# Early norms one row-block per attention round, and parts of the output projection moved into the attention drain

## What is computed

```
h = rmsnorm(x) * (1 + sc1) + sh1                      # and the same for the context
a, s, qkv = split(h @ w_in)
y = concat(short_conv(a), spatial_gating(s), neighbourhood_attention(qkv))   # 256 + 256 + 512 columns
y = group_rmsnorm(y, out_norm_g, 16 groups of 64) @ w_out
x = x + g1 * y
h2 = rmsnorm(x) * (1 + sc2) + sh2                     # then PEER: queries, top-k, experts, final norm
```

## Time and profile before

| what | value |
|---|---|
| runs of the kernel | 944.63, 945.29, 946.36 us; median 945.29 us |
| the profiled execution | 940.76 us, of it 939.0 us from the first to the last instruction |
| PE busy, PE weight load busy | 890.5 us (95%), 837.9 us (89%) |
| DVE, ACT, POOL busy | 535.4, 283.5, 257.4 us |
| mean granted TensorE clock | 0.976 of full |
| read from HBM | 290.72 MB, 311 GB/s over the span |

### The profile page before, as it was taken

How to read it: one execution, slowest core, us unless ns; L and a number is a source line. 1 busy time by engine, 2 the same in 40 slices (tenths; PEclk the granted TensorE clock), 3 DMA queues, 4 the chain that set the end, 5 groups by cost and what they waited for, 6 DMA issues and landing times.

```text
span 939.0 us, 18081 instructions
## 1 busy us (share of the span) xinstructions
PE 890.5 (95%) x6850; PEld 837.9 (89%) x6850; DVE 535.4 (57%) x1035; ACT 283.5 (30%) x687; POOL 257.4 (27%) x239
## 2 busy tenths in 40 slices
PE   5799999869999999999998999999999999999995
PEld 3587998449798999999997999999999999999995
DVE  1446104657458976997445688888434343334347
ACT  3453223664633211112113688883000000000002
POOL 0000000330133033346543233364432323222320
PEclk9597999999999999999999899999999999999998
DMA  9674583204336489999999999999999999999993
GB/s 371 289 269 171 189 314 136 89 7 175 135 135 270 119 244 384 410 409 409 409 409 410 409 362 326 320 320 353 408 409 408 409 409 409 409 409 409 409 409 131
DMA packets 73984, 292.74 MB, mean 312 GB/s; under 512 B 9026, under 2 KB 9154, under 8 KB 67396
## 3 DMA queue, kind: packets, MB, share of 16 engines
q1 hardware_dynamic: 36868, 159.67, 44.1%
q0 software_dynamic: 28416, 100.78, 28.4%
q10 hardware_dynamic: 8640, 31.46, 8.4%
HBM read 290.72 MB, written 1.05 MB: 311 GB/s over the span
## 4 chain that ended last, share of the span: by engine, by line
PE 36%; DMA 32%; DVE 5%; ACT 3%; issue 2%; POOL 1%; ACTq 0%; DVEq 0%; SPq 0%
DMA A<-in_peer_v,row_expert 25%; PE bank L830 24%; PE bank L839 4%; DMA A<-in_peer_u,row_expert 4%; DVE sum L1355 3%; DMA stage<-in_peer_u_t 2%; PE bank L573 1%; PE bank L575 1%; PE bank L574 1%; PE bank L724 1%; PE bank L727 1%; PE bank L726 1%; POOL A L1635 1%; PE bank L779 1%; PE bank L757 1%
## 5 line engine op out<-in xcount | busy, mean ns | idle before, releaser
L830 PE MATMUL bank<-A,stage 128*128 128x160 f32 x2048 | 291.3, 301 | 2.3 <-DMA stage<-in_peer_u_t 1.1
L830 PEld LDWEIGHTS bank<-A,stage 128*128 128x128 f32 x2048 | 282.0, 191 | 5.9 <-issue 5.6
L886 PE MATMUL bank<-A,stage 128*128 128x160 f32 x2048 | 278.4, 299 | 0.0
L886 PEld LDWEIGHTS bank<-A,stage 128*128 128x128 f32 x2048 | 278.2, 190 | 0.0
L1355 DVE SCALAR_TENSOR_TENSOR sum<-A,row_gate,sum 128x1024 f32<-128x1024 f32 x81 | 104.0, 1284 | 132.8 <-DMA A<-in_peer_v,row_expert 131.1
L1635 POOL DMA_INDIRECT A<-in_peer_u,row_expert x80 | 91.1, 1138 | 140.7 <-DVE row_dot L1342 133.4
L1635 POOL DMA_INDIRECT A<-in_peer_v,row_expert x84 | 82.6, 984 | 166.2 <-DVE sum L1355 148.8
L1342 DVE CUSTOM_DVE_ANT_0 A<-A 128x1024 f32<-128x1024 f32 x80 | 97.4, 1220 | 46.9 <-DMA A<-in_peer_u,row_expert 46.8
L1175 ACT ACTIVATE A<-bank 128x480 f32<-128x480 f32 x1 | 0.6, 570 | 276.3 <-PE bank L886 276.3
L1108 ACT ACTIVATE A<-bank 128x160 f32 (+1 forms) x88 | 26.7, 303 | 155.2 <-PE bank L830 155.2
L575 PE MATMUL bank<-h_hi,ring_low 128*128 128x256 f32 x256 | 73.1, 286 | 0.0
(11 more groups left out here) (234 smaller groups left out, 1240.6 us busy)
## 6 DMA issues: line engine op xcount, KB each, us to landing
stage<-in_peer_u_t SPq DMA_DIRECT2D x128, 512.0 KB, 11.1
stage<-in_peer_v SPq DMA_DIRECT2D x68, 512.0 KB, 7.7
stage<-in_peer_v ACTq DMA_DIRECT2D x60, 512.0 KB, 8.3
A<-in_ada_w SPq DMA_DIRECT2D x24, 1024.0 KB, 7.0
A<-in_w_in SPq DMA_DIRECT2D x11, 1024.0 KB, 4.8
A<-in_w_q SPq DMA_DIRECT2D x8, 1024.0 KB, 5.5
A<-in_w_out SPq DMA_DIRECT2D x4, 1024.0 KB, 6.9
stage<-in_bias_mask SPq DMA_DIRECT2D x1, 2048.0 KB, 12.7
```

The costliest lines, as they stand in the source:

```text
L830: mm = pe.matmul(o, stage[j][:, k * P:(k + 1) * P], H2[:, k, 0:ND], start=(k == 0), stop=(k == KD - 1))
L886: mm = pe.matmul(bank[b][:, n * ND:(n + 1) * ND], stage[c % SLOTS][:, m * P:(m + 1) * P], A3[:, c, :], start=(c == 0 and n == 0), stop=(c ...
```

## The change

In the attention rounds, DVE norms one row-block in each of rounds 1 to 4 instead of two in rounds 2 and 4; ACT rounds one in each of rounds 2 to 5; DVE takes one rest in each of rounds 4 to 7, two rounds behind the rounding.

In the drain, three pieces of the output projection are taken out of it and put into the list, 96 of its 192 matmuls: `out_part` 0 (k = 0, 1 for output blocks 0 to 3, 24 matmuls) ahead of `attend_pair` 6, `out_part` 1 (k = 2, 3 for the same blocks, 24) behind `turned_pair` 7, and `out_part` 2 (k = 0 to 3 for output blocks 4 to 7, 48) behind `attend_pair` 7. `group` 2 goes between `turned_pair` 7 and `out_part` 1, in another bank. `group` 3 comes behind `out_part` 2. The projection proper keeps k = 4 to 7. DVE norms blocks 4 and 5 when the last heads have been copied, blocks 6 and 7 after the reciprocal of group 3. Quarters 0 to 3, whose rests DVE makes, get a semaphore of their own.

```diff
--- before.py
+++ after.py
@@ -131,18 +131,24 @@
             steps += [("score_pair", j), ("scores", 2 * j), ("scores", 2 * j + 1)]
         if j == 0:
             turn()
+        if j == pairs:
+            steps.append(("out_part", 0))
         if 0 <= j - 2:
             steps.append(("attend_pair", j - 2))
         if 0 <= j - 1 < pairs:
             steps.append(("turned_pair", j - 1))
+        if j == pairs:
+            steps += [("group", 2), ("out_part", 1)]
         if 1 <= j <= 6:
             steps += [("quarter", 2 * j + 2), ("quarter", 2 * j + 3)]
-        if j in (3, 5):
-            steps.append(("yn", j // 2 - 1))
+        if 2 <= j <= 5:
+            steps.append(("yn_round", j - 2))
+        if 4 <= j <= 7:
+            steps.append(("yn_rest", j - 4))
         if j == 6:
             steps.append(("squares", 2))
     q0 = len(splits)
-    steps += [("squares", 3), ("group", 2), ("group", 3), ("yn", 2), ("yn", 3)]
+    steps += [("squares", 3), ("out_part", 2), ("group", 3), ("yn", 2), ("yn", 3)]
     steps += [("split", q0), ("split", q0 + 1), ("split", q0 + 2), ("w_out", 0), ("stat2", 0), ("x1_turned", 0)]
 
     ada(4 * G2)
@@ -233,16 +239,19 @@
             if n % 2 == 0:
                 put(("attend", n // 2), n // 2 % 2)
         elif kind == "group":
-            put((kind, n), 2 + n % 2)
+            put((kind, n), (2, 3, 0, 3)[n])
+        elif kind == "out_part":
+            if n != 1:
+                for m in (n, n + 1):
+                    put(("w_out", m), 4 + m)
         elif kind == "w_out":
-            for m in range(4):
-                put((kind, m), 4 + m)
+            pass
         elif kind == "stat2":
             put((kind, 0), 0)
         elif kind == "x1_turned":
             for j in range(4):
                 put((kind, j), (1, 2, 3, 7)[j])
-        elif kind in ("squares", "split", "context", "ctx_squares", "yn", "quarter", "scores"):
+        elif kind in ("squares", "split", "context", "ctx_squares", "yn", "yn_round", "yn_rest", "quarter", "scores"):
             pass
         elif kind == "keys":
             put((kind, n), 4 + n % 4)
@@ -440,7 +449,8 @@
         weight_rounded, weight_split, h_full, h_rounded, ctx_ready = map(
             sem, ("weight_rounded", "weight_split", "h_full", "h_rounded", "ctx_ready"))
         query_split = sem("query_split")
-        quarter_rounded, quarter_split = sem("quarter_rounded"), sem("quarter_split")
+        quarter_rounded, quarter_split, first_quarter_split = map(
+            sem, ("quarter_rounded", "quarter_split", "first_quarter_split"))
         yn_rounded, yn_split = sem("yn_rounded"), sem("yn_split")
         silu_zero, silu_ready, sq_ready, root_ready, h_ready, mrow_ready = map(
             sem, ("silu_zero", "silu_ready", "sq_ready", "root_ready", "h_ready", "mrow_ready"))
@@ -709,25 +719,34 @@
                 pe.matmul(o[:, :], group_ones, YS[:, 2 * j:2 * j + 2, :], start=True, stop=True)\
                   .then_inc(fill_sem(("group", j)), 1)
 
+            def out_products(k, dims):
+
+                w = [(weight_hi[splits.index(("w_out", b))], WR_lo[:, ring_of[("w_out", b)] % RING]) for b in range(4)]
+                pe.wait_ge(yn_split, k + 1)
+                for m in dims:
+                    name = ("w_out", m // 2)
+                    o = opened(pe, name) if k == 0 and m % 2 == 0 else bank[place[name][0]]
+                    oo, cc = o[:, m % 2 * T:m % 2 * T + T], slice(m % 2 * P, m % 2 * P + P)
+                    a_hi, a_lo = w[m // 2]
+                    pe.matmul(oo, a_hi[:, k, cc], yn_hi[:, k, :], start=(k == 0 and m % 2 == 0), stop=False,
+                              skip_group_check=True)
+                    pe.matmul(oo, a_hi[:, k, cc], YN_lo[:, k, :], start=False, stop=False, skip_group_check=True)
+                    mm = pe.matmul(oo, a_lo[:, k, cc], yn_hi[:, k, :], start=False, stop=(k == KD - 1),
+                                   skip_group_check=True)
+                    if k == KD - 1 and m % 2 == 1:
+                        mm.then_inc(fill_sem(("w_out", m // 2)), 1)
+
+            def out_part(i):
+
+                pe.wait_ge(first_quarter_split, 4)
+                pe.wait_ge(quarter_split, 12 if i == 2 else 4)
+                for k in range(4) if i == 2 else (2 * i, 2 * i + 1):
+                    out_products(k, range(4, KD) if i == 2 else range(4))
+
             def out_projection():
 
-
-                pe.wait_ge(quarter_split, 16)
-                w = [(weight_hi[splits.index(("w_out", b))], WR_lo[:, ring_of[("w_out", b)] % RING]) for b in range(4)]
-                for k in range(KD):
-                    pe.wait_ge(yn_split, k + 1)
-                    for m in range(KD):
-                        name = ("w_out", m // 2)
-                        o = opened(pe, name) if k == 0 and m % 2 == 0 else bank[place[name][0]]
-                        oo, cc = o[:, m % 2 * T:m % 2 * T + T], slice(m % 2 * P, m % 2 * P + P)
-                        a_hi, a_lo = w[m // 2]
-                        pe.matmul(oo, a_hi[:, k, cc], yn_hi[:, k, :], start=(k == 0 and m % 2 == 0), stop=False,
-                                  skip_group_check=True)
-                        pe.matmul(oo, a_hi[:, k, cc], YN_lo[:, k, :], start=False, stop=False, skip_group_check=True)
-                        mm = pe.matmul(oo, a_lo[:, k, cc], yn_hi[:, k, :], start=False, stop=(k == KD - 1),
-                                       skip_group_check=True)
-                        if k == KD - 1 and m % 2 == 1:
-                            mm.then_inc(fill_sem(("w_out", m // 2)), 1)
+                for k in range(4, KD):
+                    out_products(k, range(KD))
 
             def second_stat():
 
@@ -805,10 +824,12 @@
                     turned_pair(n)
                 elif kind == "attend_pair":
                     attend_pair(n)
-                elif kind in ("squares", "split", "context", "ctx_squares", "yn", "quarter", "scores"):
+                elif kind in ("squares", "split", "context", "ctx_squares", "yn", "yn_round", "yn_rest", "quarter", "scores"):
                     pass
                 elif kind == "group":
                     group_sums(n)
+                elif kind == "out_part":
+                    out_part(n)
                 elif kind == "w_out":
                     out_projection()
                 elif kind == "stat2":
@@ -1013,8 +1034,8 @@
                         act.wait_ge(ring_full[0][ring_of[name] % RING], 16 * (ring_of[name] // RING + 1))
                     act.activation(weight_hi[splits.index(name)][:, kk, :], WR[:, ring_of[name] % RING, kk, :],
                                    ACT.Copy).then_inc(quarter_rounded, 1)
-                elif kind == "yn":
-                    for k in (2 * n, 2 * n + 1):
+                elif kind == "yn_round" or kind == "yn":
+                    for k in (n,) if kind == "yn_round" else (2 * n, 2 * n + 1):
                         act.wait_ge(yn_ready, k + 1)
                         act.activation(yn_hi[:, k, :], YN[:, k, :], ACT.Copy).then_inc(yn_rounded, 1)
                 elif kind == "ctx_squares":
@@ -1195,7 +1216,7 @@
             eng.wait_ge(quarter_rounded, n + 1)
             eng.tensor_tensor(WR_lo[:, slot, kk, :], WR[:, slot, kk, :],
                               weight_hi[splits.index(name)][:, kk, :].bitcast(F32), ALU.subtract)\
-               .then_inc(quarter_split, 1)
+               .then_inc(first_quarter_split if n < 4 else quarter_split, 1)
 
         @block.vector
         def _(dve):
@@ -1240,13 +1261,11 @@
                 dve.sem_inc(free_sem(("group", j)), 1)
                 link(dve.reciprocal(roots[j % 2], roots[j % 2]))
 
-            def group_norm(j):
-                for m in range(2):
-                    k = 2 * j + m
-                    dve.scalar_tensor_tensor(YN[:, k, :], YR[:, k, :], colv[:, COL_OG + k:COL_OG + k + 1],
-                                             roots[j % 2][:, m * T:(m + 1) * T], ALU.mult, ALU.mult)\
-                       .then_inc(yn_ready, 1)
-                dve.wait_ge(yn_ready, 2 * j + 2)
+            def norm(k):
+                j, m = k // 2, k % 2
+                dve.scalar_tensor_tensor(YN[:, k, :], YR[:, k, :], colv[:, COL_OG + k:COL_OG + k + 1],
+                                         roots[j % 2][:, m * T:(m + 1) * T], ALU.mult, ALU.mult)\
+                   .then_inc(yn_ready, 1)
 
             def softmax(j):
 
@@ -1434,13 +1453,17 @@
                     if n >= 3 and n % 2 == 1:
                         attended((n - 3) // 2)
 
-                    if n in (2, 4):
-                        group_norm(n // 2 - 1)
+                    if 1 <= n <= 4:
+                        norm(n - 1)
                 elif kind == "squares" and n == 3:
                     attended(3)
+                    norm(4)
+                    norm(5)
                 elif kind == "group":
                     group_reciprocal(n)
-                    group_norm(n)
```

(7 more changed lines are left out.)

## The result

| | before | after |
|---|---|---|
| median of seven runs each, first session | 944.63 us (942.31 to 946.36) | 937.89 us (935.25 to 939.67) |
| ratio of the runs | | 0.9945, 95% interval 0.9928 to 0.9961 |
| profiled execution, and its span | 940.76 us, 939.0 us | 937.84 us, 936.1 us |
| mean granted clock of the profiled execution | 0.976 | 0.976 |

The change makes the kernel faster, by 5.2 us according to the ratio; with its interval the ratio gives 3.7 to 6.8 us, and the two medians lie 6.7 us apart. The two profiled executions differ by 2.9 us, close to the 3.1 us of the forecast, but the median of 937.89 us lies under the range that was given (939.5 to 946.0 us). So there are two questions: whether the walk through the queues is right, and where the rest comes from.

A forecast was written before the change was run, and what follows sets the result against it. The prediction took the ACT-DVE loop as the bound before the projection and PE inside it. 5.1 us saved less 2.0 us of clock took 940.76 to 937.7 us; 4.5 us to the median gave 942.2, range 939.5 to 946.0.

The forecast's parts named there:

- the walk through the queues: Engine queues from attention rounds to statistics: 5.1 us saved, 2.0 us lost to the clock, -3.1 us in sum.
- Part 1, the rounds: Attention rounds: spreading norms and rests removes ACT's wait, so round 7's first exponential starts 6.2 us earlier.
- Part 2, the drain: Drain on PE: with the moved projection pieces, the last attend ends at 206.2 us and group 3 at 212.5.
- Part 3, the gap: Before the projection's second half: PE idles 5.6 us for rest 4; statistics at 230.0 us, 5.1 us saved.
- The clock: Behind PE's new gap: the clock falls to 0.50 and costs 2.0 us; idles of 2.29 us and less are harmless.
- The level: Whole kernel: the profiled execution's 937.7 us was raised 4.5 us to a median of 942.2 us.
- The clock holds: Rival behind PE's new gap: clock stays up or is low only briefly, 940.2 us; chance 0.15.
- POOL takes the rounds back: Rival in the rounds: rests and norms meet POOL pairs, 2 to 4 us lost, 945.2 us; chance 0.22.
- The slower case: Rival: pieces moved into the drain while rounds get no shorter; 3.0 us later with the clock, 948.3 us; chance 0.08.
- More than the walk: Rival: the old clock dip at 190 us also cost the rounds, up to 1 us more saved, 939.2 us; chance 0.05.

The follow-up runs named there:

- e2: The drain change alone, norms and rests in pairs as before, against the kernel before: ratio 1.0018, 1.7 us over before.
- e6: The kernel before again, unchanged, for a third profile: 72.83 us from first scores to statistics.
- e10: The rounds change alone, drain and projection as before, second run, against the kernel before: ratio 0.9927, median 935.03 against 942.0 us.
- e7: The changed kernel again, unchanged, for a second profile, against the kernel before: ratio 0.9964, 937.5 against 941.59 us.
- e9: The changed kernel again, unchanged, in a third session, against the kernel before: ratio 0.9942, 937.08 against 942.0 us.
- e5: The kernel before again, unchanged, for a second profile, against itself: ratio 1.0011.
- e1: The rounds change alone, drain and projection as before, first run, against the kernel before: ratio 0.9929, median 935.2 against 941.79 us.
- e4: The changed kernel plus 40 useless matmuls in the gap before the projection's second half; ratio to the kernel before 0.9943, 935.91 us.
- e11: The changed kernel plus 40 useless matmuls in the gap, second run; ratio to the kernel before 0.9941, 936.43 us.

## Why the prediction was wrong, point by point

**Part 1, the rounds: right in mechanism and in size.** From the first exponential of round 1 to that of round 7 I had 25.2 us. In the profile after the change it is 197.30 - 171.44 = 25.86 us, and the exponential of round 7 came 5.45 us earlier than before instead of 6.2. But 0.57 of the missing 0.66 us lie in round 1 alone, which took 175.89 - 171.44 = 4.45 us instead of 3.88 beside the low clock at 171 to 175 us. The four profiles of any kernel with a low clock in this round (after, e2, e6, e10) have 4.40 to 4.45 us, the ten without it 3.88 or 3.89. e7 and e9 are among the ten, and in both the same distance is 25.26 us. ACT's timeline in e9:

```profile
171.28 0.69 ACT L1074 ACTIVATE A<-bank,nmax 128x512 f32<-128x512 f32 x1 [2.05 <-DVE nmax L1274]
...
196.54 0.67 ACT L1074 ACTIVATE A<-bank,nmax 128x512 f32<-128x512 f32 x1
```

The scaling under POOL, one in each round, did not lengthen the rounds beyond that sum. This part alone is worth 6.1 us in the first stretch, 6.7 to 6.9 us in time.

The Trainium skill, page "SBUF — State Buffer", section "Who interferes with whom", would have locked the norms and rests behind a GpSimd pair as well. In the trace after the change none of them stands behind one: the rests at 187.26 and 191.84 us start before POOL's pairs at 187.88 and 192.06. The rule isn't contradicted, it had no occasion; the scaling under the pair agrees with it, 1.03 us against 0.49.

**Part 2, the drain: right.** The last attend ended at about 207.3 us (206.2 worked out), group 3's sum began at 213.23 (212.0), both 1.1 to 1.2 us late: 0.8 us of it is the late start of round 7. In e9, without that, PE still resumes 22.5 us behind the first exponential of round 7, where 21.6 had been worked out; half of these 0.9 us lie ahead of the fourth group sum and half behind it. The reciprocal of group 2 did hold up the copy of the last heads, at 209.28 us, and `out_part` 2 covered it.

**Part 3, the gap: right.** 5.53 us against 5.6.

**The clock: a step that failed.** Two of its sentences have to be told apart. The price behind the new gap was taken as 2.0 us and is 1.2 to 2.3. But "Idles of 2.29 us and less leave it at 1.00" was read from one execution and is false: behind 2.30 us (e5) and 2.29 us (e1) it fell, behind 2.29 us (before, as shown) and 2.30 us (e10) it didn't, nor behind 2.85 us at 189.57 us in e6. So the drain before the change costs 1.2 to 2.2 us more in other executions than in the one shown (first stretch 72.83 and 73.77 against 71.59 us), and the change takes these idles away. I had booked the clock as a cost of the new kernel alone; it is a saving too. The shift is 72.7 - 69.2 = 3.5 us in the means of three profiles each, against 3.1 forecast and 2.6 in the pair of the first profiles. That 3.5 is so close to 3.1 is in part luck: against the profile from which it was worked out the changed kernel gained 71.6 - 69.2 = 2.4 us, 0.7 less than forecast, and 1.1 us came from the side of before.

By the Trainium skill, page "TensorE: Matmul & The Clock Gate", Part 1, the point at which the clock changes differs from run to run of one kernel, because its monitor doesn't start with the kernel. The pairs of equal idles above agree with that; a single trace can't say whether an idle of 2 to 3 us is free.

**The level: the term that was mis-sized.** The sum gave 937.7 us for the profiled execution of the changed kernel, and that execution took 937.84 us. To reach a median the prediction added 4.5 us, the distance of the median of three runs of before (945.29) from its one profiled execution (940.76). The changed kernel's median, 937.89 us, lies only 0.05 us above its profiled execution. So this added term is the whole of the 4.3 us between 942.2 and 937.89 us, and it is what put the time outside the range. The later sessions show it too: the medians of before are 944.63 us in the first session and then 941.79, 941.59 (942.57 in e5's own runs), 942.0 and 941.29, so 0.5 to 1.8 us above 940.76 instead of 4.5, while the changed kernel has 937.89, 937.5 and 937.08 us. Of such a distance the clock explains about 1.1 us, by which the profile shown has a shorter first stretch than the mean of before. Why before was some 3 us slower in the first session alone, where the three runs come from, no run shows; this cause stays open.

Told by the difference of the two kernels, the miss is made up as follows. The three runs shown had a median of 945.29 us, the seven of the first session 944.63; 0.7 us of the miss is that. From it and 3.5 us one gets 941.1 us, still inside the range. To the 5.2 us of the first session's ratio, whose interval reaches 1.5 us to either side, 1.7 us are missing, and 1.5 us more lie between that ratio and the 6.7 us of the two medians. The three sessions give 5.2, 3.4 and 5.5 us, a mean of 4.7; the first stretch explains 3.5 of it. The column to the end is 0.7 us shorter in the changed kernel's profiles (623.1 against 623.8 in the mean), but its spread inside one kernel is 3.1 us. Whether the remaining 1.2 us is chance or a small effect in the expert stream is open.

**The rivals.** "The clock holds" was wrong, it fell in all three profiles. "POOL takes the rounds back" was wrong. The slower case describes e2, 1.7 us over before where 3.0 had been worked out. "More than the walk" came closest and had the smallest chance. Its kind of reason, old low stretches that vanish, was right, but the stretch that it named, at 190 us in the rounds, was not the one that counted: in e6 it is absent, and the first exponentials of rounds 1 and 7 are still 31.33 us apart, against 31.45. It should have been priced by more than the one dip in the trace. The chances add up to 0.74 for faster, not 0.73 (0.50, 0.15, 0.05 and a fifth of 0.22). The range's lower end was set by the single profile plus half a microsecond of spread; the spread of the runs themselves was already 1.7 us with three of them.

## What to carry to other kernels

Work moved under a drain pays only as far as the chain behind it doesn't start later: here the fourth group sum stood behind 5.8 us of moved matmuls, and its reciprocal, norms and rests then left PE idle; putting the rests that were ready ahead of it, and one query rest behind the reading that followed, gave about 3 us more than the change itself (7.3 and 7.7 us by the ratios, against a mean of 4.7). Before counting a removed wait in full, follow the next engine's queue until something waits again. And where a difference is a few microseconds, take two or three profiles of the kernel before, and charge a clock that falls behind idles to both kernels. The distance between one profiled execution and a median of other runs is not a constant that can be carried from one kernel to the next: it was 4.5 us in the runs of before shown and 0.05 us after the change.

## What the runs showed of the hardware

Behind the same idle of 2.3 us the granted clock of TensorE falls to 0.50 in some executions (e1, e5) and stays at 1.00 in others (e10, and before as shown). Behind the gap of 5.53 us it was at 0.50 in all four profiles that have one (the changed kernel's three and e2). At 0.50 eight transposes take 1.97 us instead of 1.09 us, and the 16 matmuls of the statistics 6.19 instead of 3.83 us. Matmuls that serve nothing, put into a gap of 5.5 us, kept the clock at 1.00 in both profiles (e4, e11), and they cost PE nothing that it needed.
